# A two-block transformer on one core: the first block's attention steps placed by a table, and w_mod's rows moved

## What is computed

```python
mod_x = split(silu(c) @ w_mod[l] + b_mod[l], 6)       # mod_c from c_ctx
hx = adaln(x, norm1_g[l], mod_x[0], mod_x[1])         # hc from ctx, mod_c
mix_x, mix_c = token_mixing(hx, hc, ...)              # below
x = x + mod_x[2] * mix_x
hx = adaln(x, norm2_g[l], mod_x[3], mod_x[4])
x = x + mod_x[5] * channel_mix(hx, ...)               # l=0: swiglu FFN; l=1: experts
# ctx likewise, in layer 0 only

# token_mixing: q, k, v, mlstm q/k/v/o and 16 gate columns = h @ w_in
#  att: softmax over a window and the context, with a sink, 8 heads
#  mlstm: conv(5) + silu on q, k; gates: cumsum of log_sigmoid, running
#  maximum; two directions; chunk-wise memory; sigmoid(o_pre) gate
#  out = concat(norm(att), norm(mlstm) * sigmoid(o_pre)) @ w_out
```

## Time and profile before

| what | us |
|---|---|
| median of 3 runs | 2511.64 (2508.62 to 2514.37) |
| the profiled execution, its own time | 2519.33 |
| its span, first to last instruction | 2517.2 |
| layer 0, end of the gate projection to the memory stage | 100.7 to 258.8 |
| layer 0, memory stage | 258.8 to 312.1 |
| layer 0, w_out | 312.1 to 369.0 |
| layer 1, end of the gate projection to the memory stage | 798.7 to 908.3 |

### The profile page before, as it was taken

The page is one execution under the profiler, slowest core; times in us unless marked ns, Lnnn a source line. Parts: engine busy times, 40 slices in busy tenths (PEclk is TensorE's granted clock), DMA queues, the critical chain, the costliest instruction groups (busy, mean ns, idle before and its releaser), DMA issues.

```text
span 2517.2 us, 33928 instructions
## 1 busy us (share of the span) xinstructions
PE 2447.4 (97%) x13485; PEld 1994.0 (79%) x13485; DVE 1816.5 (72%) x2875; ACT 1312.0 (52%) x1992; POOL 66.5 (3%) x71
## 2 busy tenths in 40 slices
PE   7999999999999988999999999999999999999998
PEld 2565647788786777888888888888899999989998
DVE  6788627677432564999999999999777775676774
ACT  3135514222233453877778778777645554545553
POOL 0000010000010000000000000000000000000000
PEclk8999999999999999999999999999899999999999
DMA  7532024555322103989889889898643445433452
GB/s 288 209 111 99 1 84 150 185 199 197 142 77 79 57 17 114 358 335 366 332 333 366 332 329 363 338 366 331 261 168 118 153 182 202 151 134 134 169 183 100
DMA packets 71653, 510.71 MB, mean 203 GB/s; under 512 B 7905, under 2 KB 9057, under 8 KB 10049
## 3 DMA queue, kind: packets, MB, share of 16 engines
q1 hardware_dynamic: 68690, 500.21, 53.4%
q10 hardware_dynamic: 2208, 6.32, 0.7%
q0 software_dynamic: 592, 1.97, 0.2%
HBM read 506.23 MB, written 2.23 MB: 202 GB/s over the span
## 4 chain that ended last, share of the span: by engine, by line
PE 85%; DVE 9%; ACT 4%; issue 1%; DMA 1%; POOL 0%; ACTq 0%; DVEq 0%
PE bank L815 84%; DVE UL L2089 2%; DVE arena L2097 2%; ACT UH L1606 1%; ACT arena L1609 1%; PE bank L1188 1%; DMA consts<-in_c 1%; DVE arena L2093 1%; DVE small L2156 1%; PE bank L930 0%; DVE arena L2089 0%; DVE XT L2097 0%; DVE arena L2789 0%; ACT L1609 0%; ACT XT L1609 0%
## 5 line engine op out<-in xcount | busy, mean ns | idle before, releaser
L2089 DVE TENSOR_TENSOR UL<-ring,UH 128x1024 fp32r<-128x1024 f32 (+1 forms) x804 | 970.0, 1218 | 321.4 <-ACT UH L1606 301.3
L1606 ACT CAST UH<-ring 128x1024 fp32r<-128x1024 f32 (+1 forms) x804 | 830.3, 1040 | 562.0 <-PE bank L815 514.4
L815 PE MATMUL bank<-XH,UH 128*128 128x256 f32 x1040 | 302.6, 291 | 6.1 <-DVE UL L2089 3.4
L815 PE MATMUL bank<-XL,UH 128*128 128x256 f32 x1040 | 294.7, 283 | 0.0
L815 PE MATMUL bank<-XH,UL 128*128 128x256 f32 x1040 | 294.7, 283 | 0.0
L815 PE MATMUL bank<-UH,HGh 128*128 128x512 f32 (+1 forms) x768 | 291.3, 379 | 3.2 <-issue 2.4
L815 PE MATMUL bank<-UH,HGl 128*128 128x512 f32 (+1 forms) x768 | 288.0, 375 | 0.0
L815 PE MATMUL bank<-UL,HGh 128*128 128x512 f32 (+1 forms) x768 | 287.0, 374 | 0.0
L2136 DVE CUSTOM_DVE_ANT_0 JUNK<-ring,CROW 128x1024 bf16<-128x1024 f32 x176 | 206.3, 1218 | 14.1 <-ACT CROW L1609 10.0
L815 PEld LDWEIGHTS bank<-XH,UH 128*128 128x128 f32 x1040 | 199.7, 192 | 15.0 <-issue 6.5
L815 PE MATMUL bank<-HT,ring 128*128 128x512 f32 (+2 forms) x576 | 206.5, 514 | 1.7 <-ACT HT L1609 1.7
(11 more groups left out here) (217 smaller groups left out, 4021.6 us busy)
## 6 DMA issues: line engine op xcount, KB each, us to landing
ring<-in_w SPq DMA_DIRECT2D x477, 1024.0 KB, 4.9
XT<-in_x ACTq DMA_DIRECT2D x2, 1024.0 KB, 12.1
bias_scratch<-BIAS POOLq DMA_DIRECT2D x6, 192.0 KB, 2.1
consts<-in_c ACTq DMA_DIRECT2D x1, 1109.0 KB, 8.2
out_y<-XT ACTq DMA_DIRECT2D x2, 512.0 KB, 3.5
BIAS<-bias_scratch POOLq DMA_DIRECT2D x1, 768.0 KB, 7.0
constd<-in_c ACTq DMA_DIRECT2D x1, 768.0 KB, 4.1
consts<-in_c ACTq DMA_DIRECT2D x1, 512.0 KB, 17.7
```

The lines of the kernel that those rows point to most:

```text
L815: return e.matmul(out, lhsT, rhs, start=start, stop=stop, skip_group_check=True)
L1606: return e.copy(out, in_)
L2089: return e.tensor_tensor(out, a, b, op)
```

## The change

The rate is replaced by the table BESIDE, so many attention steps beside each projection of cp, vm and om: in layer 0 (2, 2, 2, 3), eight times 2, and four times 3, which are all 37; in layer 1 1 each beside cp and vm, then 2, 2, 2, 3, which are all 21. There is no tail. From vm on each attention step is followed by two REST steps in layer 0 and by three in layer 1. gate_out now stands right behind om3 and its copy, and directly ahead of the memory stage. In layer 0 one pump instead of two stands behind each projection (17 from q to om), two stand ahead of the residual of each of wo4 to wo7 (8), and 55 beside the FFN: 44 beside f1 and f3 and 11 beside f2. The gain of norm 2 is computed with its own chunk (m = 39) instead of at m = 47; the residuals behind w_out wait for their own chunk (m = 23) instead of the gain, and those behind the FFN wait for theirs (m = 47).

```diff
--- before.py
+++ after.py
@@ -20,7 +20,8 @@
 FF = 2816
 NF = FF // 128
 NEG = -1.0e30
-ATT_RATE = (1.3, 0.8)
+BESIDE = ({"cp": (2, 2, 2, 3), "vm": (2,) * 8, "om": (3, 3, 3, 3)},
+          {"cp": (1, 1, 1, 1), "vm": (1,) * 8, "om": (2, 2, 2, 3)})
 EPS = 1e-6
 LN_EPS = 1e-5
 ALPHA = (2.0 * 2) ** 0.25
@@ -253,22 +254,19 @@
     out.append(("turned", 1))
     for l in range(2):
         out.append(("mix", l))
-        acc, i_att, rest = [0.0], [0], list(REST)
+        i_att, rest = [0], list(REST)
         n_att = (32 if l == 0 else 16) + 5
 
         def more():
-            for _ in range(min(l + 1, len(rest))):
+            for _ in range(min(l + 2, len(rest))):
                 out.append(("rest", l, rest.pop(0)))
 
-        def beside(with_rest):
-            acc[0] += ATT_RATE[l]
-            while acc[0] >= 1:
-                acc[0] -= 1
-                if i_att[0] < n_att:
-                    out.append(("att", l, i_att[0]))
-                    i_att[0] += 1
-                    if with_rest:
-                        more()
+        def beside(what, j):
+            for _ in range(BESIDE[l][what][j]):
+                out.append(("att", l, i_att[0]))
+                i_att[0] += 1
+                if what != "cp":
+                    more()
 
         def project(kind, *name, **more):
             if kind == "gemm":
@@ -276,7 +274,7 @@
             else:
                 tok(*name, key="w_in", idx=(l,), **more)
             if l == 0:
-                pump(2)
+                pump(1)
             out.append(("evict", name))
 
         if l == 0:
@@ -290,37 +288,29 @@
             out.append(("rope", l, m))
         tok("va", l, key="w_in", idx=(l,), c0=640, w=128, n=4)
         if l == 0:
-            pump(2)
+            pump(1)
         out.append(("swap", l))
         project("gemm", "gate", l, c0=2304, M=16)
         for j in range(4):
-            beside(False)
+            beside("cp", j)
             project("gemm", "cp", l, j, c0=768 + 128 * j)
-        acc[0] = 0.0
         for part in range(2):
             out.append(("tokw", ("vm", l, part), [((("vm", l, part), k), "w_in", (l,), [(128 * k, 1280 + 256 * part, 256)])
                                                   for k in range(8)]))
             for tb in range(4):
                 out.append(("vm", l, part, tb))
-                beside(True)
+                beside("vm", 4 * part + tb)
             if l == 0:
-                pump(2)
+                pump(1)
         for m in range(4):
-            beside(True)
+            beside("om", m)
             project("gemm", "om", l, m, c0=1792 + 128 * m)
-        if l == 0:
-            while todo[0][0] == 0:
-                pump(1)
         out.append(("gate_out", l))
-        while i_att[0] < n_att:
-            out.append(("att", l, i_att[0]))
-            i_att[0] += 1
-            more()
-        while rest:
-            out.append(("rest", l, rest.pop(0)))
         out.append(("memory", l))
         for m in range(8):
             gemm("wo", l, m, key="w_out", idx=(l,), c0=128 * m)
+            if l == 0 and m >= 4:
+                pump(2)
             out.append(("evict", ("wo", l, m)))
         if l == 0:
             out.append(("ffn",))
@@ -2143,7 +2133,7 @@
                     w.wait_ge(*vec.now())
                     tt(md, md, par(f"bmod{l}", m0, 8).unsqueeze(2).to_broadcast([128, 8, 2]),
                        ALU.add).then_inc(*vec.up(("mod", l, m)))
-                    if m == 47:
+                    if m == 39:
                         gain(l, "n2g", 4)
                     if m == 15 and l == 1:
                         gain(1, "n1g", 1)
@@ -2633,7 +2623,7 @@
                     ts(bg, par(f"bg{l}", 0, 1, 16), 1.0 / 15.0, None, ALU.mult).then_inc(*vec.up(("bg", l)))
                 elif kind == "evict" and st[1][0] == "wo":
                     l, m = st[1][1], st[1][2]
-                    w.wait_ge(*vec.at("gain", l, "n2g"))
+                    w.wait_ge(*vec.at("mod", l, 23))
                     residual(st[1], l, m, 2, 256 * l, ("wo", l, m))
                 elif kind == "vm":
                     _, l, part, tb = st
@@ -2690,6 +2680,7 @@
                         tt(gl, G[:, k + 1, :], gh.bitcast(F32), ALU.subtract).then_inc(*vec.up(("stage", k + 1)))
                     split_low(unit(st[2][0][0])[0])
                 elif kind == "ffn_end":
+                    w.wait_ge(*vec.at("mod", 0, 47))
                     for m in range(8):
                         residual(("f2", m), 0, m, 5, 0, ("f2", m))
                 elif kind == "route":
```

## The result

The changed kernel takes **2708.17 us** (median of 4 runs, 2707.53 to 2709.38), the kernel before 2513.01 in the runs beside it (4 runs, 2508.62 to 2522.07): ratio 1.077, 95% interval 1.0744 to 1.0795. It is slower by 195 us, far outside the predicted range of 2501 to 2527. The span of the profiled execution grew from 2517.2 to 2705.8 us, by 188.6.

A forecast was written before the change was run, and what follows sets the result against it. TensorE (busy 97%) was taken as the bound, with 32 us winnable by placement. Terms 0.3 + 3.9 + 1.7 + 1.2 - 5.8 + 3.8 = +5.1 us on the median 2511.64 gave 2516.7 us, range 2501 to 2527.

The forecast's parts named there:

- Part 4: Eight pumps beside w_out: hidden, but f1's second tile loads late, delaying the root of norm 2: +1.7 us.
- Part 5: Rest of the pumps: FFN up keeps 44, w_2 gets 11 instead of 2, slightly delaying low parts: +1.2 us (0 to +3).
- Part 2: Layer 0's attention steps beside the projections: PE's sum stays 136 us, waits bring the stretch to 158.4 against 158.1: +0.3.
- one wait of 9.6 us for the clear: Layer 0's vm part: PE idle 9.6 us for ACT's copy of tile 9's transposes, queued behind POOL's clear.
- The 4.1 for em: Layer 0's vm part: em on ACT follows step 20's exponential, so PE waits from 60.6 to 64.8, 4.1 us.
- one such penalty, 2.8 us: Layer 0's vm part: slower PE matmuls on the next projection after the long idle, 2.8 us lost.
- Part 3: Layer 0's gate_out sigmoids and table loads on ACT now directly precede the memory stage, delaying its first exponential: +3.9 us.
- rival A: Slower: PE idle at both memory stage starts and before layer 1's vm4 brings half clock; +13.2, 2525 us; chance 0.21.
- Part 6: Layer 1: stretch before the memory stage falls from 109.6 to 103.8 us, -5.8; sigmoid tables ahead of its memory stage, +3.8.
- Part 1: Up to layer 0's gate 14 pumps become 7; PE has no gap there, so 0.
- the sum of +5.1: Whole kernel: all parts' terms added, +5.1 us, giving 2516.7 us.

The follow-up runs named there:

- the first experiment: Changed kernel with half a slot of padding ahead of the first f1 and again at layer 1's queries, same list of steps: 2531.85 us.
- seven: Changed kernel with half-slot padding, gate_out ahead of the last three attention steps and the gates' chain at the old pace: 2526.17 us.
- five: Changed kernel with half-slot padding, last om projection and gate_out moved ahead of the last three attention steps: 2534.49 us.
- six: Changed kernel with half-slot padding, one chain item (layer 1 two) behind each attention step instead of two (three): 2530.29 us.
- ten: Changed kernel's table without padding, gate_out ahead of the last three steps, chain at the old pace, pumps spread as in nine: 2520.26 us.
- nine: Kernel before, own steps, no padding; pumps respread: pairs up to the gate, one per cp, none beside vm/om, pairs beside wo3-wo7, 8 beside w_2: 2515.85 us.
- four: Changed kernel with all pumps back where the kernel before has them, which restores its packing; the table stays: 2530.47 us.
- eight: Kernel before with its own steps, but the changed kernel's pump placement and the half-slot padding: 2516.48 us.

## Why the prediction was wrong

**The step that failed** is in parts 4 and 5, that "the ring's slots are repacked" and that "FFN up keeps 44". I followed the new packing to f1's second tile, priced its one late load at 1.7 us, and then took FFN up as unchanged because its pumps and its work are. The packing holds for every slot of FFN up, and the same question (what releases the slot that the look-ahead asks for at this step?) has there a worse answer: the pump just executed. It costs 164 us in FFN up, and 11.1 instead of 2.6 (the first experiment's 163.8 against 161.2) in the stretch behind it. The numbers to see it were there: a load takes 4.9 us and a half tile 5.7, so that a load that is released only as the half tile that needs it begins, and has a cast and a split behind it, is on the path. None of my rivals had this mechanism; the slower one had the clock. The prediction did name its own test, "if a stretch after layer 1 changes, something here is not local"; the stretch that changed lies before.

**Part 4's price itself was right.** The cast of f1's second tile and norm 2's root behind it, ACT's timeline of the changed kernel:

```profile
383.18 1.04 ACT L1596 CAST UH<-ring 128x1024 fp32r<-128x1024 f32 x1 [1.60 <-DMA ring<-in_w]
384.13 0.20 ACT L1599 ACTIVATE tokens<-tokens 128x4 f32<-128x4 f32 x1
```

The root starts 6.13 us after w_out's end at 378.0, for which 6.15 stood in the sum. The stretch lost 3.1 instead of 1.7; its clock was 0.61. The pumps beside w_out were hidden (56.7 us, DVE 35.2 busy).

**Part 2** said +0.3 and got +6.6. PE's own sum was right, 136 against the 138 above. The places were right in part, the sizes were not. PE's idle groups of this stretch in the changed kernel, from its timeline:

```profile
146.06 0.44 PE L920 MATMUL bank<-consts,arena 128*128 128x128 f32 x2 [2.51 <-DVE arena L2083]
147.88 0.91 PE L805 MATMUL bank<-arena 128*64 128x128 f32 x8 [1.38 <-ACT arena L1596]
154.26 5.74 PE L805 MATMUL bank<-ring,HT 128*128 128x256 f32 x16 [1.97 <-DVE arena L2143]
164.22 2.64 PE L805 MATMUL bank<-arena,consts 16*4 16x512 f32 x4 [3.58 <-ACT arena L1667]
...
198.43 6.14 PE L805 MATMUL bank<-consts,arena 128*128 128x4 f32 x32 [2.67 <-ACT arena L1599]
```

I had one wait of 9.6 us for the clear. It did not come: PE's longest idle time, 3.58 us, ended at 164.22, released by the exponential that ACT does behind the convolution's silu, and the clear, from 161.95 to 165.46, held up ACT's copy by 1.14 us and PE not at all. The 4.1 for em came as 2.67. But the waits are spread over 50 us, and three stretches of half clock come with them (about 148 to 158, 166 to 171 and 200 to 205 us): the vm part from 154.26 needs 5.74 us for 256 columns where the earlier trace rows give 3.45. I had counted one such penalty, 2.8 us; the clock took 13.2 of the stretch against 9.5 before. The sum had 19.8 us of idle time (4.7, 0.6, 9.6, 4.1 and 0.8), and 13.7 came. So the idle time was overrated and the clock underrated. The table also loses against its own variant with the slower chain (seven against five: 4.3 us of idle and 5.6 of clock), and so in six against the first, so the pace of two items is part of it; the remainder (ten against nine: 4.8 of clock, no idle, in one execution of each) I did not take apart.

**Part 3** was right in its mechanism: ACT's timeline at the head of layer 0's memory stage.

```profile
264.73 1.28 ACT L1599 ACT_TABLE_LOAD   x1
266.02 2.19 ACT L1599 ACTIVATE arena<-arena 128x512 f32<-128x512 f32 x4
268.23 1.28 ACT L1599 ACT_TABLE_LOAD   x1
269.52 0.58 ACT L1599 ACTIVATE arena<-bank,small 128x384 f32<-128x384 f32 x1
```

The first exponential starts 5.6 us after the stage (263.93), as written, and the stage is 4.0 longer for +3.9. In the kernels traced it takes 57.3 to 60.3 us with gate_out directly ahead of it (changed, first, four, six), 55.0 to 55.5 with the last three steps between (five, seven, ten), and 52.8 to 53.3 in the order of before (before, eight, nine). So 1.9 or more of the 4.0 are shown to be this; the other part, which stays with the table, is not explained. In layer 1 the same delay (1096.47 less 1091.94, 4.5, as written) cost 6.3 and not 3.8: 2.1 more idle than before, and a clock of 0.88 where it had been 1.00. That is rival A's mechanism, a gap of 3.7 us at the stage's start and half clock behind it:

```profile
1097.53 2.52 PE L805 MATMUL bank<-arena 128*128 128x129 f32 x10 [3.70 <-DVE arena L2087]
```

**Part 5** (+1.2, bounds 0 to +3): 2.6 in the first experiment and 3.6 in the eighth; nine has 8 pumps beside w_2 instead of 11 and still 3.4 (788.5 less 623.9 against 161.2). **Part 6** said -5.8 for layer 1's stretch and got -3.5, between its bounds. **Part 1**, nothing up to the gate, got -1.5, which shows nothing: the six kernels traced with the same steps and pumps up to there end the gate projection between 97.8 and 102.3 us.

Without the lock step the sum of +5.1 stands against a measured +19.6 (the first experiment's median less 2512.27 for the kernel before in the runs beside it). By the profiled spans it is +10.7 (2527.9 less 2517.2), since the profiled execution of before was a long one, 7.7 above its median. Of the 19.6 the table alone gives 18.2 (the fourth) and the moved pumps alone 4.1 (the eighth). Even without the lock step the truth lay above the range, 2531.9 against 2527, on rival A's side.

## What to carry to other kernels

When a stream of mixed pieces is packed into slots of a ring, adding or moving one piece can turn the halves of every slot behind it. So ask at each stage, not only at the place of the edit: which slot does the look-ahead reach at this step, whose last piece frees its place in the ring, and how long before the need was that piece used? If it was used by the same engine just before, load, cast and consumer run one after the other. A deeper look-ahead can be the cause: one unit less was as good as the padding. And where PE has gaps, add up idle time and clock apart, and know how your traced execution lies among the others: here it was 7.7 us above the median, more than most of the differences that were looked for.

## What was not expected of the hardware

A 1 MB load takes about as long in either rhythm: 4.7 to 4.9 us in the lock step, where the DMA engines are busy 0.30 of the time, and 4.9 as the median of the kernel before, whose FFN up has them busy 0.51 of the time. No load made up for its late start. The clock is not fixed by the code: the first experiment and the changed kernel have the same steps in layer 0's memory stage, and one took 60.3 us at 0.89, the other 57.3 at 0.97.

```profile
260.86:321.20 60.34, 54.05 (x266) 39.52 (x265) 34.45 (x127) 37.40 (x115) 2.49 (x2) 0.89 0.05 18
```

Nor is it fixed for one kernel: among the runs of the kernel before beside the ninth and tenth, the fastest, 2509.20 us, has a mean granted clock of 0.984 and the slowest, 2522.19 us, 0.978. That difference of clock is 15 us of the length, and the difference of time is 13.

The Trainium skill, "TensorE: Matmul & The Clock Gate", Part 1, has activity release the throttle. The trace agrees for the tile above: the clock fell while PE stood idle, from 563.4 to 568.34, and came back while PE worked, by 575. So with 4.9 us idle in every tile of 18.9 (107.6 and 415.5 by 22) the mean of FFN up is 0.86, where a clock halved throughout would read 0.5.
